# Suffix sums of a stick-breaking attention, grouped by PSUM bank, and a last row finished in halves

## What is computed

```python
# attention of one head, s < t strictly
z         = q.k / sqrt(128)
log_keep  = where(mask, log_sigmoid(-z), 0)
log_after = cumsum(log_keep, reverse) - log_keep          # suffix sums over the keys
a         = where(mask, exp(log_sigmoid(z) + log_after), 0)
y_a       = (a @ v) * silu(gate_a)
# mixer: trailing means over 2, 4, 8, 16 tokens minus the token, a linear map, a scale
y_b       = multiscale_pool(u) * silu(gate_b)
out       = concat(y_a, y_b) @ W_out
x         = x + out * rsqrt(mean(out * out) + eps) * post_gain
```

## Time and profile before

| | |
|---|---|
| Median of 3 runs | 718.9 us (718.89 to 719.06) |
| The profiled execution | 718.82 us, span 717.1 us |
| Mean granted clock of TensorE | 0.997 |
| TensorE busy | 707.3 us (99%) |
| VectorE, ScalarE, POOL busy | 584.4, 434.5, 72.2 us |
| Share of TensorE in the chain that ended last | 95% |

### The profile page before, as it was taken

One profiled execution on the slowest core, in us unless ns is written; L12 is line 12 of the kernel. 1 busy time (PEld: TensorE's weight loads), 2 busy tenths in 40 slices (PEclk: granted clock), 3 DMA queues, 4 the chain that ended last, 5 costly groups with the idle time before them and its releaser, 6 DMA issues.

```text
span 717.1 us, 9879 instructions
## 1 busy us (share of the span) xinstructions
PE 707.3 (99%) x3740; PEld 610.9 (85%) x3740; DVE 584.4 (81%) x750; ACT 434.5 (61%) x577; POOL 72.2 (10%) x93
## 2 busy tenths in 40 slices
PE   8999999999999999999999999999999999999995
PEld 6888888988888898888888888888888888888884
DVE  3499987988798888898897978898888984376787
ACT  4764576566776656766766676756678434253461
POOL 0000000200020110011110011020000000001000
PEclk9999999999999999999999999999999999999998
DMA  8965446576646666655766666657655307468986
GB/s 293 393 195 146 119 116 181 144 175 193 181 123 167 176 175 178 158 151 151 201 139 176 177 158 170 169 134 181 173 172 176 118 22 242 118 176 229 280 314 234
DMA packets 38831, 128.59 MB, mean 179 GB/s; under 512 B 4352, under 2 KB 5376, under 8 KB 37888
## 3 DMA queue, kind: packets, MB, share of 16 engines
q1 hardware_dynamic: 31728, 102.78, 42.2%
q0 software_dynamic: 6912, 25.17, 20.4%
q10 hardware_dynamic: 144, 0.01, 0.0%
HBM read 123.74 MB, written 4.19 MB: 178 GB/s over the span
## 4 chain that ended last, share of the span: by engine, by line
PE 95%; DVE 2%; issue 1%; DMA 1%; ACT 0%; POOL 0%; DVEq 0%; SPq 0%; POOLq 0%; ACTq 0%
PE ps L1866 36%; PE ps L1874 19%; PE ps L1810 11%; PE ps L1777 9%; PE ps L1778 9%; PE ps L1776 9%; PE ps L1914 1%; PE ps L1912 1%; DVE mix L1683 1%; DMA raw<-w_v 1%; DVE mix L1586 0%; PE ps L1803 0%; PE ps L1801 0%; DVE mix L1614 0%; DVE mix L1583 0%
## 5 line engine op out<-in xcount | busy, mean ns | idle before, releaser
L1866 PE MATMUL ps<-a_ops,w_hi 128*128 128x512 f32 x1120 | 270.8, 391 | 0.0
L1866 PEld LDWEIGHTS ps<-a_ops,w_hi 128*128 128x128 f32 x1120 | 205.1, 188 | 39.6
L658 ACT ACTIVATE w_hi<-raw 128x1024 fp32r<-128x1024 f32 x155 | 163.6, 1055 | 69.6 <-PE ps L1866 40.2
L1108 DVE TENSOR_TENSOR raw_lo<-raw,w_hi 128x1024 fp32r<-128x1024 f32 x155 | 188.7, 1223 | 20.7 <-ACT w_hi L658 19.8
L1874 PEld LDWEIGHTS ps<-a_ops,raw_lo 128*128 128x128 f32 x1120 | 145.7, 191 | 6.3
L1874 PE MATMUL ps<-a_ops,raw_lo 128*128 128x256 f32 x1120 | 149.9, 283 | 0.0
L1731 POOL DMA_DIRECT2D raw<-w_heads x40 | 34.9, 874 | 313.6 <-DMA raw<-w_heads 260.2
L1776 PE MATMUL ps<-w_hi,a_ops 128*128 128x512 f32 x160 | 62.3, 390 | 0.0
L1778 PE MATMUL ps<-w_hi,a_ops 128*128 128x512 f32 x160 | 62.3, 389 | 0.0
L1777 PE MATMUL ps<-raw_lo,a_ops 128*128 128x512 f32 x136 | 53.0, 389 | 0.0
L1557 DVE TENSOR_TENSOR raw_lo<-raw,w_hi 128x1024 fp32r<-128x1024 f32 x23 | 28.2, 1225 | 25.7 <-ACT w_hi L1011 25.7
(11 more groups left out here) (222 smaller groups left out, 1033.2 us busy)
## 6 DMA issues: line engine op xcount, KB each, us to landing
raw<-w_heads SPq DMA_DIRECT2D x100, 512.0 KB, 4.2
raw<-w_heads POOLq DMA_DIRECT2D x40, 512.0 KB, 5.6
raw<-w_out SPq DMA_DIRECT2D x35, 512.0 KB, 4.8
raw<-w_v SPq DMA_DIRECT2D x15, 512.0 KB, 10.0
x_rows<-x SPq DMA_DIRECT2D x6, 1024.0 KB, 11.7
mix<-xT SPq DMA_DIRECT2D x16, 256.0 KB, 10.0
raw_more<-w_out SPq DMA_DIRECT2D x6, 512.0 KB, 6.6
out<-mix SPq DMA_DIRECT2D x6, 512.0 KB, 2.7
```

Of the source, the lines that this page charges most:

```text
L658: act.activation(hi_slot(g), raw_slot(raw, slot), ACT.Copy).then_inc(w_hi_done, 1)
L1108: dve.tensor_tensor(raw_slot(raw_lo, slot), raw_slot(raw, slot), hi_slot(g).bitcast(F32), ALU.subtract).then_inc(w_split, 1)
L1866: mm = pe.matmul(dst, hi[:, k * P:(k + 1) * P], a_ops[:, a:a + SEQ], start=k == 0 and p in (0, 1, 5), stop=stop and k == KH - 1, skip_grou ...
```

## The change

Suffix sums: TensorE first adds each bank's own part with neg_tri (bank 0, bank 1 with tiles 1 and 3 together, tile 2), then tile 3 onto tile 2, and then for heads 0 to 6 the later tiles of tile 1 (256 columns, tiles 2 and 3) and of tile 0 (384 columns, tiles 1 to 3), each from a sum that VectorE and ScalarE prepared. ScalarE copies the first 128 columns of each sum, VectorE adds the rest. The sum for tile 1 stays over p1_neg; the one for tile 0 uses first_sum, which lies where mixed_lo and work lie, with mixed_hi for its rounded part. Therefore copy_out of product 0 at r = 0 moves behind the exp of the weights, and u_window_of of an even pool tile waits for the logits.

Last row: its final pass has two pieces instead of four. POOL computes the root of the sum of the other three squares (with D * EPS), VectorE puts it into the PSUM column behind the last tile, and ScalarE squares 513 columns with a scale of D ** -0.5, so that the accumulator holds the mean square itself; the tensor_scalar of the last row is gone. The preparation of both tail rows now comes ahead of row 0's final pass.

```diff
+            first_sum = sb("first_sum", [P, WIDTH[1]], scope=heads)
...
+        later = {1: (later_sum[:, :], later_hi[:, :], later_lo[:, :]),
+                 0: (first_sum[:, :], mixed_hi[:, 0:WIDTH[1]], mixed_lo[:, 0:WIDTH[1]])}
...
+            def later_copy_of(h, u):
...
+                act.wait_ge(softplus_masked, 2 * h + 2)
+                if h:
+                    act.wait_ge(pool_done, h + h % 2)
+                act.activation(later[0][0][:, 0:P], tri[:, START[1]:START[1] + P],
+                               ACT.Copy).then_inc(later_copied, 1)
+                act.wait_ge(folded, 3 * u + 2)
+                act.activation(later[1][0][:, 0:P], tri[:, START[2]:START[2] + P],
+                               ACT.Copy).then_inc(later_copied, 1)
...
-                act.wait_ge(later_summed, 2 * h + 2)
-                act.activation(later_hi[:, :], later_sum[:, :], ACT.Copy).then_inc(later_hi_done, 1)
+                act.wait_ge(later_copied, 2 * h + 2)
+                for n, b in enumerate((1, 0)):
+                    act.wait_ge(later_summed, 2 * h + n + 1)
+                    act.activation(later[b][1], later[b][0], ACT.Copy).then_inc(later_hi_done, 1)
...
-                    if p in (1, 2, 3):
+                    if p in (1, 2, 3) and not (p == 1 and r == 0 and i > 0):
                         copy_out(u, p - 1)
...
                             if p == 1:
                                 gate_sigmoid(h0 - 1, 0)
                                 weights_exp_of(h0 - 1)
+                                copy_out(u, 0)
...
+                            later_copy_of(h0, u)
                             softplus_hi_of(h0)
...
+                if (s, dc) == (LAST_ROW, 2):
+                    act.wait_ge(root_set, 1)
+                    act.activation(cumsum[:, 0:BANK + 1], last_tile, ACT.Square, scale=float(D) ** -0.5,
+                                   accum_out=out_ms[:, s:s + 1]).then_inc(rows_squared, 1)
...
-                dve.tensor_tensor(later_sum[:, :], tri[:, START[1] + P:START[1] + WIDTH[1]],
-                                  tri[:, START[2]:START[2] + WIDTH[2]], ALU.add).then_inc(later_summed, 1)
+                second, first = later[1][0], later[0][0]
+                dve.tensor_tensor(second[:, P:], tri[:, START[2] + P:START[2] + WIDTH[2]],
+                                  tri[:, START[3]:START[3] + P], ALU.add).then_inc(later_summed, 1)
+                if h:
+                    dve.wait_ge(pool_done, h + h % 2)
+                dve.wait_ge(later_copied, 2 * h + 2)
                 dve.wait_ge(later_summed, 2 * h + 1)
-                dve.tensor_tensor(later_sum[:, P:HALF], later_sum[:, P:HALF],
-                                  tri[:, START[3]:START[3] + P], ALU.add).then_inc(later_summed, 1)
+                dve.tensor_tensor(first[:, P:], tri[:, START[1] + P:START[1] + WIDTH[1]], second,
+                                  ALU.add).then_inc(later_summed, 1)
...
-                dve.wait_ge(later_hi_done, h + 1)
-                dve.tensor_tensor(later_lo[:, :], later_sum[:, :], later_hi[:, :].bitcast(F32),
-                                  ALU.subtract).then_inc(later_ready, 1)
+                for n, b in enumerate((1, 0)):
+                    dve.wait_ge(later_hi_done, 2 * h + n + 1)
+                    dve.tensor_tensor(later[b][2], later[b][0], later[b][1].bitcast(F32),
+                                      ALU.subtract).then_inc(later_ready, 1)
...
+                if z % 2 == 0:
+                    dve.wait_ge(logits_done, z + 1)
...
+            rows_gain(s, 2)
+            dve.wait_ge(root_ready, 1)
+            dve.wait_ge(rows_free, rows_count(0, 3))
+            dve.tensor_copy(beside, row_root).then_inc(root_set, 1)
+            row_final(s)
+            rows_gain(LAST_ROW, 2)
+            row_final(LAST_ROW)
...
+            pool.wait_ge(out_summed, 6)
+            pool.wait_ge(half_set, 1)
+            pool.tensor_tensor(row_root, out_ms[:, LAST_ROW:LAST_ROW + 1], half,
+                               ALU.pow).then_inc(root_ready, 1)
+            row_rstd(2, TAIL_ROWS[0])
...
-                for b in range(TT):
-                    for later in range(b, TT if b or h == HEADS - 1 else 1):
...
+                for a, z in ((0, BANK), (BANK, 2 * BANK), tri_part(2)):
+                    sums(neg_tri, a, z, tri_hi[:, a:z], tri_lo[:, a:z])
+
                 if h == HEADS - 1:
...
+                    pairs = [(b, n) for b in (0, 1, 2) for n in range(b + 1, TT)]
+                else:
+                    pairs = [(2, 3)]
+                for b, n in pairs:
+                    a, z = tri_part(b, n - b)
+                    src, end = tri_part(n)
+                    mm = sums(neg_ones, a, z, tri_hi[:, src:end], tri_lo[:, src:end])
+                if h < HEADS - 1:
+                    for n, b in enumerate((1, 0)):
+                        a, z = tri_part(b, 1)
+                        pe.wait_ge(later_ready, 2 * h + n + 1)
+                        mm = sums(neg_ones, a, z, later[b][1], later[b][2])
+                mm.then_inc(logits_done, 1)
```

More of the change, by code:

```diff
@@ L186, in hybrid_layer @@
         neg_not_first = sb("neg_not_first", [P, 1])
+        half, row_root = ms_col[:, 0:1], ss_col[:, 0:1]
         with ExitStack() as values:
@@ L232, in hybrid_layer @@
         mixed_hi = sb("mixed_hi", [P, SEQ], F32R)
+        with ExitStack() as heads:
+            first_sum = sb("first_sum", [P, WIDTH[1]], scope=heads)
         mixed_lo = sb("mixed_lo", [P, SEQ], F32R)
@@ L315, in hybrid_layer @@
         softplus_ready = sem("softplus_ready")
+        later_copied = sem("later_copied")
         later_summed = sem("later_summed")
@@ L369, in hybrid_layer @@
         c11_done = sem("c11_done")
+        half_set = sem("half_set")
+        root_ready = sem("root_ready")
+        root_set = sem("root_set")
         tail_loaded = [sem(f"tail_loaded{s}") for s in TAIL_ROWS]
@@ L383, in hybrid_layer @@
         FINAL_PIECES = 2
-        def final_pieces(s):
-            n = 2 * FINAL_PIECES if s == TAIL_ROWS[-1] else FINAL_PIECES
-            return [(i * D // n, (i + 1) * D // n) for i in range(n)]
+        FINAL = [(i * D // FINAL_PIECES, (i + 1) * D // FINAL_PIECES) for i in range(FINAL_PIECES)]
+        LAST_ROW = TAIL_ROWS[-1]
+        beside = ps[:, (ACC + 2) * BANK:(ACC + 2) * BANK + 1]
+        last_tile = ps[:, (ACC + 1) * BANK:(ACC + 2) * BANK + 1]
         def rows_part(s, a, b):
@@ L622, in _ @@
             for s in ROW_ORDER:
-                for a, b in final_pieces(s):
+                for a, b in FINAL:
                     stored += 1
@@ L795, in softplus_hi_of @@
                 act.activation(tri_hi[:, :], tri[:, :], ACT.Copy).then_inc(softplus_hi, 1)
+            def later_copy_of(h, u):
+                if h == HEADS - 1:
+                    return
+                act.wait_ge(softplus_masked, 2 * h + 2)
[6 more added lines that the diff above has]
+                               ACT.Copy).then_inc(later_copied, 1)
             def later_hi_of(h):
@@ L942, in _ @@
                                 o_hi_of(0)
+                            later_copy_of(h1, u)
                             softplus_hi_of(h1)
@@ L1033, in rows_square @@
                 junk = work[:, :]
-                if (s, dc) == (0, 3):
+                if (s, dc) == (LAST_ROW, 2):
+                    act.wait_ge(root_set, 1)
+                    act.activation(cumsum[:, 0:BANK + 1], last_tile, ACT.Square, scale=float(D) ** -0.5,
+                                   accum_out=out_ms[:, s:s + 1]).then_inc(rows_squared, 1)
+                elif (s, dc) == (0, 3):
                     act.activation(junk, src, ACT.Square, scale=not_first[:, 0:1],
@@ L1634, in _ @@
                     late_lo_of(q)
+            dve.memset(half, 0.5).then_inc(half_set, 1)
             dve.wait_ge(rows_gain_loaded, 16)
@@ L1695, in _ @@
                                   ALU.add).then_inc(out_summed, 1)
[L1696 to L1702, removed]
+            s = TAIL_ROWS[0]
+            dve.wait_ge(out_summed, 6)
+            dve.wait_ge(rows_squared, rows_count(s, 2))
+            dve.tensor_scalar(out_ms[:, s:s + 1], out_ss[:, 4 * s + 3:4 * s + 4],
+                              out_ms[:, s:s + 1], 1.0 / D, ALU.add,
+                              ALU.mult).then_inc(out_ms_ready, 1)
+            rows_gain(s, 2)
[5 more added lines that the diff above has]
+            row_final(LAST_ROW)
         @block.gpsimd
@@ L1768, in row_rstd @@
                                    ALU.pow).then_inc(out_rstd_ready, 1)
-            for n, s in enumerate(ROW_ORDER):
-                row_rstd(n, s)
+            row_rstd(0, ROW_ORDER[0])
+            row_rstd(1, ROW_ORDER[1])
+            pool.wait_ge(out_summed, 6)
[3 more added lines that the diff above has]
+            row_rstd(2, TAIL_ROWS[0])
+            pool.wait_ge(rows_squared, rows_count(LAST_ROW, 2))
```

(7 more changed lines are left out.)

## The result

The changed kernel takes 721.25 us (720.82 to 721.57) against 719.19 us (718.89 to 719.76) for the kernel before, 10 runs each: ratio 1.0028, 95% interval 1.002 to 1.0036. It is 2.1 us slower. The profiled execution has a span of 719.6 us.

What follows compares the result with a forecast made beforehand. TensorE was taken as the bound up to the tail. On 718.8 us, odd heads +2.6, even heads -0.8, head 7 -0.1 and the tail -0.6 gave +1.1: 719.9 us (720.0 on the median), range 718.0 to 721.8.

Steps and rivals of the forecast that it cites:

- The bound and what TensorE saves: Suffix sums: TensorE bounds up to the tail; 0.45 us saved per head 0 to 6, 0.1 on head 7.
- Odd heads: Heads 1, 3, 5: product 2 waits for the late copy into work, 0.87 us later each, +2.6 us in all.
- that cover: VectorE's sums: ScalarE's second copy ends near 199.7, second sum starts 199.72, so no delay; any lateness hits VectorE's chain.
- Even heads: Heads 0, 2, 4, 6: VectorE's extra 0.47 us delays weights_lo; weighted values start only 0.2 earlier, -0.8 us in all.
- The tail: Last rows: no tensor_scalar -0.3, two pieces -0.26, stores 0; sum -0.6 us, with the new power just hidden.
- The sum: Whole kernel: +2.6 - 0.8 - 0.1 - 0.6 = +1.1 us, giving 719.9 us.
- (a): Whole kernel: copy's wait on odd heads, small gain on even ones; 719.0 to 721.0 us, chance 0.60.
- (b): Same waits but shorter: copy ends 0.3 us earlier, even heads keep 0.45 each; about 718 us, chance 0.18.
- (c): Odd heads: copy ends before 210.0, product 2 never waits, full saving arrives; 715.0 us, chance 0.07.
- slower than 720.3: Outcome class for the measured time: a third of (a) and all of (d) and (e), chance 0.35.
- (d): Suffix sums: 128-column copies come late and push VectorE, 0.5 us more on seven heads; 723.3 us, chance 0.12.
- (e): TensorE: the waits bring the clock to half rate behind three long waits, 8.4 us; 728 us, chance 0.03.

Runs made afterwards that it cites:

- e3: Changed kernel, but at r = 0 ScalarE waits for the logits and copies product 0 before gate_sigmoid and weights_exp: 717.6 us, ratio 0.9984.
- e6: Kernel before, with only the copy of product 0 at r = 0 moved behind gate_sigmoid and weights_exp: 720.31 us, ratio 1.0012.
- e4: Changed kernel, but for even heads VectorE makes weights_lo before the rest of product 4's weights: 719.68 us, ratio 1.0012.
- e5: Changed kernel, copy before gate_sigmoid, even heads' weights_lo before rest of product 4's weights, odd heads' product 6 combining before rest of product 1's weights: 716.28 us.
- e9: Changed kernel with gate_logsig of an odd head moved ahead of the weight sum that stood before it: 719.87 us, ratio 1.0011.
- e8: Kernel of e5, with gate_logsig behind the rest of product 2's weights and weights_exp ahead of gate_sigmoid: 715.14 us, ratio 0.995.

## Why the prediction was right, and where its terms were off

**The bound and what TensorE saves.** Right. The sums of an even head went from 2.42 to 1.98 us (0.44 saved, 0.45 forecast; 0.43 to 0.46 in the kernel without breaks), head 7 saved 0.11 (0.1 forecast). The estimate of 0.12 a head, worked out from the formula of the Trainium skill, page "TensorE: Matmul & The Clock Gate", section "Back-to-back issue gap", was too low here; the rows were the right guide.

**Odd heads.** The mechanism was right and is shown: the wait carries the name of the copy, it goes when the copy is moved ahead (e3), and it appears in the kernel before when the copy is moved behind (e6). The term was +0.87 and measured +0.97. The step that was mis-sized is the one that priced the copies of 128 columns at nothing for VectorE. Their row:

```profile
199.98 0.29 DVE L1341 TENSOR_TENSOR later_sum<-tri 128x128 f32<-128x128 f32 x1
200.41 0.43 DVE L1347 TENSOR_TENSOR first_sum<-tri,later_sum 128x256 f32<-128x256 f32 x1
```

```profile
199.98 0.31 ACT L823 ACTIVATE later_sum<-tri 128x128 f32<-128x128 f32 x1
```

The copy takes 0.31, not 0.27, and VectorE starts 0.12 after its end, not 0.02. The second sum starts 0.43 after the first instead of the 0.33 reckoned, and all of VectorE behind it is 0.1 later: the rest of the softplus stands 1.74 ahead of the sums' start instead of 1.85. With the 0.46 of the new rest (0.47 forecast) gate_logsig is 0.58 later against the sums. The prediction had called that cover thin. The prediction also missed product 1's wait for the combining (0.18 and a restart); it cost nothing here, because product 2 waits for something else anyway, but it became a term in e3, where odd heads took 0.12 of a possible 0.44.

**Even heads.** The mechanism was right and is shown by e4. The term was -0.2 a head, measured -0.07 to -0.10; the same 0.1 of the copies accounts for it (tri_lo of the weights is 0.56 later against the sums' start, not 0.47). Four heads gave -0.35 instead of -0.8. The forecast also expected the list of waits to name weights_lo four times; the list has no such entry, and the break shows only between starts.

**The tail.** -0.6 forecast, -0.62 measured. Its parts were -0.3, -0.26 and 0 and are -0.25 and -0.37. The new power did push row 0's last pass so far that the product with the gain starts late, at 713.10. It ends at 713.79, after POOL's power (713.68), and so not POOL but this product releases the last pass ([0.19 <-DVE mix L1632] above): the new power was not quite hidden. The halves take 2.48 instead of 2.74, and the remaining 0.11 of the 0.37 lies behind them, in the last store.

**The sum.** Forecast +1.1, by the same parts in the trace +1.8, timed +2.1 (1.4 to 2.6 by the interval). Of the 0.7 between forecast and trace, 0.3 are odd heads, 0.4 even heads. The 0.3 that remain are within the interval and within the scatter of the start; nothing here assigns them. The measured 721.25 lies inside the range of 718.0 to 721.8, but near its upper end, just outside the 719.0 to 721.0 of (a), and in the class (slower than 720.3) that had a chance of 0.35. The direction and the mechanism were right; the forecast difference was about half of the measured one.

**The rivals.** (b), a shorter wait, and (c), no wait, are refuted by the rows. (d), late copies, was right in kind and not in size: they make VectorE later by 0.1 instead of 0.5, and the sums do not wait for them. (Its 723.3 should read 723.4: 719.9 and seven times 0.5.) (e), the clock, did not happen: three breaks of 1.1 us left the clock row at nine tenths or more throughout, and the mean granted clock at 0.998.

## What to carry to other kernels

When the bound engine gets less work, ask at once what it would next wait for. Here 3 us of saving were real, and three waits in the changed kernel, none over 1.1 us, took them and more; a fourth showed when these were gone (e5) and a fifth in another order (e9). The kernel of e8 has none of the five and not one instruction less, only another order. A buffer shared to save memory turns into a place in a queue: the copy only had to follow the sums, and the change put it behind the exp as well. If an operation must wait for an event, put it right behind that event and not behind other work of its engine. Price a wait between engines with a hop (0.06 to 0.15 us in these traces) and a restart (0.07 to 0.11) on top of the durations, and count those on every head.

## What the runs showed of the hardware

After a wait, TensorE's second matmul comes late too. In every break around the heads, in all these traces, it is 0.31 to 0.34 us from start to start for 512 columns instead of 0.23, and 0.19 for 256 columns instead of 0.12.

POOL's mask is slower beside VectorE. The two instructions of an even head's weights take 1.60 us in the trace before and 2.60 in the changed kernel; those of an odd head's weights take 1.62 before, 1.63 in the changed kernel, 3.26 in e8 and 3.82 in e9, all with the same shape. Over all 32 the mean went from 848 to 974 ns without a change of the instruction:

```profile
L1775 POOL TENSOR_SCALAR_AFFINE_SELECT tri<-tri 128x256 f32<-128x256 f32 x32 | 30.5, 974 | 142.8 <-DVE tri L1331 78.2 <-ACT tri L836 64.6
```

Laid against VectorE's instructions, the 384 mask instructions of the twelve traces fall into two groups. In 120 of them VectorE is idle or reads PSUM, and all of these take 0.40 to 0.41 us. In the other 264 it runs for at least a part an instruction with both inputs in SBUF, and they take 0.40 to 2.91; in the trace of e9 VectorE does so from 207.99 to 212.08 and again from 212.27. The Trainium skill, page "SBUF — State Buffer", section "Who interferes with whom", says that a VectorE instruction with two SBUF inputs contends with a GpSimd instruction that reads SBUF. The rows agree, with 0.40 to 0.41 against up to 2.91. No run here takes VectorE's instruction or the mask away alone, so the shared port as the cause is argued and not shown.
